# A two-layer hybrid block on one core: half-angle root in the recurrence, head 0 scored behind the last query slab, a semaphore for each half of a low part

## The chip, the cores and the metric

The kernel runs on one core of one Trainium2 chip. The metric is the device time of one execution in microseconds, lower is better; the time before is the median of 3 runs.

## The reference

Two layers over a sequence of 256 tokens and a context of 256 tokens, width 1024, all in fp32. Each layer modulates the RMS norm of its input, multiplies by one wide matrix, feeds four branches and merges them, then applies a SwiGLU feed-forward. The second layer carries only the 256 tokens through most of its work, since its context output is not needed.

```python
def _rglru_gates(u, wa, ba, wx, bx, lam):
    r = sigmoid(blockwise(u, wa) + ba);  i = sigmoid(blockwise(u, wx) + bx)
    log_a = -LRU_C * softplus(-lam) * r
    a = exp(log_a)
    b = sqrt(-expm1(2.0 * log_a)) * (i * u)
    return a, b                                   # then a linear scan h = a*h + b, both ways

def _window_attention(q, k, v, kc, vc, sink):     # 8 heads, 2 kv heads, blocks of 128, window 128
    p = softmax([local scores, context scores, sink])
    return p_local @ v + p_ctx @ vc
...
ys = (short_conv(...) @ w_a_out, attention(...) @ w_b_out,
      (gelu(r_g) * rec) @ w_c_out, conformer_conv(d_v, d_g) @ w_d_out)
out = (sum over n of sigmoid(gate_n) * ys_n) @ w_out
x = x + gt1 * out;  x = x + gt2 * swiglu(modulate(x))
```

## The kernel before

All matrices arrive as a stream of slabs of 1 MB: 128 partitions x (8 row tiles x 2 column tiles x 128). A layer has 104 slabs, in stages named c_in (8 slabs), kv (2), q (4), d_in (8), c_out, b_out, a_cu (8 each), a_b (4), a_out, d_out (8 each), w_out (4), then ff_in and ff_out in three parts. Slabs alternate between two slots `s`; `m` counts pairs.

Each fp32 product is made of three reduced-precision ones (fp32r). ScalarE copies the raw slab in two halves into a high part `WH` (`high`, semaphore `hi_done`), GpSimd (`low`, L416) or VectorE (`low`, `lows`) subtracts it from the raw slab into a low part `WL` (semaphore `lo_done`), and TensorE adds WH*HH, WH*HL and WL*HH (`products`, L441). A slab is 48 such matmuls, over 512 columns in the first layer, over 256 in most of the second. The slot of the raw slab is free for the next load when both halves of its low part are done. GpSimd makes both halves in every stage of the first layer and in the stages of `POOL_WHOLE`; elsewhere in the second layer GpSimd makes the first half and VectorE the second. In c_in VectorE makes both. `begin(m, s, halves)` is TensorE's wait before a slab: for one or both halves of the low part, and until the PSUM banks 2s and 2s+1 have been read (`slab_out`). With halves=1 the second half is waited for at k = 4 of the first tile. `in_order` allows halves=1 only where one engine makes both halves, since both raised one semaphore.

At the start, 8 slabs of modulation weights are loaded into buffers that are still free (S, S, RAW, TMP, G, G, CD, CD). TensorE turns each pair into modulation rows and columns and then runs two row tiles of slab 0.

In c_in, each slab gives a head of the recurrence (`front`: convolution and GELU). `gates(n)` multiplies by the gate matrices (8 plain fp32 matmuls). ScalarE then makes, over 512 columns, four Tanh for the gates, and `decays(n)`: Tanh, Exp and Exp again of multiples of the decay argument; VectorE forms (e+1)*tanh (`rests`), ScalarE its root (`roots`, which needs another activation table), VectorE two products, two scans (`scans`, L1415) and the output.

In kv and q, keys and queries are rotated: TensorE applies ROT to a copy (`rotate`, into banks 4 to 7), VectorE multiplies by cosine (`cosines`, which also frees the slab's banks) and sine (`turned`). The last head's scans (`scans(KC - 1)`) stand on VectorE ahead of the cosines of query slab 0.

In d_in, one head of attention runs beside each slab. TensorE's slab of 16 steps (3 matmuls each) is cut by a list: `("t0", 6)` puts the transposes of unit 0 after step 6, `o0` its product with V, `n0` the scores of unit 0 of the next head. Unit 0 and 1 are the two query blocks, unit 2 the context (first layer only). VectorE makes the maxima (`maxima`), sums and the scaling of the probabilities (L1180), ScalarE the exponentials (`probs`), the copies of the transposes, then at the slab's end the copy of the head's result, a Tanh and `high` of the slab after next. TensorE's `turn(n, 0)` (L681) waits for the scaling.

In a_out of the second layer, the layer norm of branch d runs between the pairs: mean and variance on TensorE, subtractions, scalings and gates on VectorE and ScalarE; its result is split into high and low parts (`z_low`) during the last pair.

Of the kernel before, what the change touches and what calls it, by code (L numbers as in the profile page):

```python
# [14 lines left out]
P = 128  # L15
# [55 lines left out]
POOL_WHOLE = ("c_in", "kv", "q", "d_in", "c_out", "b_out", "a_cu", "a_b", "a_out", "w_out")  # L71
# [34 lines left out]
ATTENTION = [[("t0", 6), ("t1", 9), ("o0", 9), ("t2", 13), ("o1", 13), ("n0", 14), ("o2", 16)],  # L106
# [16 lines left out]
def build(nc, stream, modw, lruw, xT, cT, prm, rope, consts, outT):  # L123
    with ExitStack() as ctx:
# [27 lines left out]
        LC = sb("LC", 3 * 16)  # L152
# [82 lines left out]
        lo_done = [sem(f"lo_done{s}") for s in range(2)]  # L235
# [13 lines left out]
        def stage_sems(l):  # L249
# [11 lines left out]
            st("lam_v", "pos den inv z z2 p6 p5 p4 p3 p2 p1 p0 log sp c0 c1 c2 hb")  # L261
# [7 lines left out]
            st("ci_a", "r0 r1 i0 i1 t0 t1 a0 a1 e0 e1")  # L269
# [78 lines left out]
        def _(sp):  # L348
# [22 lines left out]
            for l in range(DEPTH):  # L371
# [40 lines left out]
        def _(pool):  # L412
            def low(m, s, h):
# [3 lines left out]
                    .then_inc(lo_done[s], 1)  # L417
# [21 lines left out]
        def _(pe):  # L439
# [3 lines left out]
            def begin(m, s, halves=2):  # L443
                pe.wait_ge(lo_done[s], 2 * m + halves)
                pe.wait_ge(slab_out[s], m + 1)

            def second_half(m, s):
                pe.wait_ge(lo_done[s], 2 * m + 2)

            def in_order(l, name, first):  # L450

                i = [x for x, _ in STAGES].index(name)
                if first:
                    l, name = (l, STAGES[i - 1][0]) if i else (l - 1, STAGES[-1][0])
                return l <= 0 or name in POOL_WHOLE
# [41 lines left out]
            def stage(l, name, ops, nk=KC, before=None, pairs=None, ready=None):  # L497
# [5 lines left out]
                def pair(i, start):  # L503
                    for s in range(2):
                        slots = []
                        if start >= skip:
# [3 lines left out]
                             halves=1 if in_order(l, name, start == 0) else 2)  # L510
# [43 lines left out]
            def stage_and_sums(l, name, nk, before, after, nm, w, wo):  # L554

                b = pair_base(l, name)
                for n in range(4):
# [4 lines left out]
                         halves=1 if in_order(l, name, i == 0) else 2,  # L562
# [38 lines left out]
            for l in range(DEPTH):  # L601
# [26 lines left out]
                def rotate(st_a, st_p, n, s):  # L628
                    for t in range(2):
# [4 lines left out]
                        mm(bank(4 + 2 * s + t, NX), ROT, KR[t][:, 0:NX] if st_a is a["kv_a"] else QR[s][t], True, True).then_inc(st_p.sem, 1)  # L634
# [19 lines left out]
                b = pair_base(l, "q")  # L654
                slab(b, 0, [(H, W), (H, W)], halves=1)
                for n in range(1, 4):
# [1229 lines left out]
```

## Time and profile before

| | |
|---|---|
| median of 3 runs | 2160.63 us (2160.46 to 2161.41) |
| profiled execution | 2154.54 us, span 2152.7 us |
| TensorE matmul busy | 2072.0 us, 96% |
| TensorE weight load busy | 1720.3 us, 80% |
| VectorE, ScalarE, GpSimd busy | 1125.2, 907.0, 823.5 us |
| mean granted TensorE clock | 0.993 |
| HBM read | 275.80 MB |

The span is from the first to the last instruction; the execution's own time is 1.8 us longer. In a row of the timeline the first number is the start, the second the duration; the bracket at its end is the idle time of the engine ahead of it and what released it. Durations of a group of instructions overlap a little, so the start of the next row says more on pace than the sum. A granted clock of 1.00 is 2.4 GHz, of 0.50 1.2 GHz.

### The profile page before, as it was taken

How to read it: one execution, taken by the hardware profiler on the slowest of the kernel's cores; microseconds unless marked ns; L12 is line 12 of the kernel's file. 1: busy time of each engine (PE TensorE's matmuls, PEld its weight loads, DVE VectorE, ACT ScalarE, POOL GpSimd, SP SyncE). 2: the span in 40 equal slices, each digit the busy share in tenths (PEclk: the TensorE clock that was granted, in tenths of full speed). 3: DMA queues.
4: the chain of work that ended last, by engine and by line, in shares of the span. 5: the costliest groups of instructions: out<-in, count | busy, mean ns of one | idle time of the engine just before them, and what ended most of it. 6: DMA issues, size and time to landing. Idle time of an engine off the chain costs nothing.

```text
span 2152.7 us, 30915 instructions
## 1 busy us (share of the span) xinstructions
PE 2072.0 (96%) x11836; PEld 1720.3 (80%) x11836; DVE 1125.2 (52%) x2021; ACT 907.0 (42%) x1424; POOL 823.5 (38%) x348
## 2 busy tenths in 40 slices
PE   6999889999999999999999999999999999999997
PEld 4778677788877778776777778776889999899997
DVE  6894354577789532123111111489745886444555
ACT  4895333322222332233222212379755434544434
POOL 1003221344434334332333344400445887644443
PEclk9999999999999999999999999999999999999999
DMA  8212111222222222654534422421223555344443
GB/s 332 79 59 98 59 43 56 79 98 88 88 98 90 87 78 104 236 218 176 225 120 173 156 96 81 155 77 71 108 100 120 177 190 187 146 174 157 178 176 137
DMA packets 38699, 278.37 MB, mean 129 GB/s; under 512 B 4416, under 2 KB 4416, under 8 KB 5312
## 3 DMA queue, kind: packets, MB, share of 16 engines
q1 hardware_dynamic: 38592, 276.87, 35.1%
q8 instruction: 76, 1.25, 0.2%
q14 instruction: 31, 0.25, 0.0%
HBM read 275.80 MB, written 1.05 MB: 129 GB/s over the span
## 4 chain that ended last, share of the span: by engine, by line
PE 79%; DVE 9%; ACT 7%; issue 2%; DMA 2%; POOL 1%; SPq 0%; DVEq 0%; ACTq 0%; POOLq 0%
PE PS L441 76%; PE PS L524 2%; ACT WH L769 2%; DVE PS L1177 1%; ACT S L769 1%; DVE SM L1180 1%; ACT TMP L769 1%; ACT L769 1%; PE PS L681 1%; DVE WL L1174 1%; DVE ZL L1174 1%; ACT CD L769 1%; POOL WL L416 1%; DMA RAW<-in_stream 1%; DMA S<-in_modw 1%
## 5 line engine op out<-in xcount | busy, mean ns | idle before, releaser
L416 POOL TENSOR_TENSOR WL<-RAW,WH 128x1024 fp32r<-128x1024 f32 x344 | 823.3, 2413 | 1313.3 <-ACT WH L769 1313.3
L441 PE MATMUL PS<-HH,WH 128*128 128x512 f32 (+1 forms) x2272 | 807.7, 355 | 19.3 <-DVE HL L1177 7.3
L441 PE MATMUL PS<-HL,WH 128*128 128x512 f32 (+1 forms) x2272 | 780.2, 343 | 0.0
L441 PE MATMUL PS<-HH,WL 128*128 128x512 f32 (+1 forms) x2272 | 779.7, 343 | 0.0
L769 ACT ACTIVATE WH<-RAW 128x1024 fp32r<-128x1024 f32 x416 | 417.4, 1052 | 666.1 <-PE PS L441 626.4
L441 PEld LDWEIGHTS PS<-HH,WH 128*128 128x128 f32 x2272 | 430.2, 189 | 96.5 <-issue 30.0
L441 PEld LDWEIGHTS PS<-HL,WH 128*128 128x128 f32 x2272 | 430.5, 190 | 59.5 <-issue 7.9
L441 PEld LDWEIGHTS PS<-HH,WL 128*128 128x128 f32 x2272 | 429.7, 189 | 56.0
L441 PE MATMUL PS<-ZH,WH 128*128 128x512 f32 (+1 forms) x992 | 339.4, 342 | 10.7 <-DVE ZL L1174 7.1
L441 PE MATMUL PS<-ZL,WH 128*128 128x512 f32 (+1 forms) x992 | 336.1, 339 | 0.0
L441 PE MATMUL PS<-ZH,WL 128*128 128x512 f32 (+1 forms) x992 | 336.1, 339 | 0.0
L1177 DVE SCALAR_TENSOR_TENSOR PS<-G,PRM,PS 128x512 f32<-128x512 f32 (+1 forms) x464 | 254.5, 616 | 0.2
L441 PEld LDWEIGHTS PS<-ZH,WH 128*128 128x128 f32 x992 | 187.4, 189 | 39.1 <-DVE ZL L1174 9.0
L441 PEld LDWEIGHTS PS<-ZH,WL 128*128 128x128 f32 x992 | 187.3, 189 | 22.7
L441 PEld LDWEIGHTS PS<-ZL,WH 128*128 128x128 f32 x992 | 187.5, 189 | 22.0
L1174 DVE TENSOR_TENSOR TMP<-TMP,PS 128x512 f32<-128x512 f32 (+1 forms) x56 | 31.6, 564 | 291.4 <-ACT TMP L769 276.8
L769 ACT ACTIVATE TMP<-PS 128x256 f32<-128x256 f32 (+1 forms) x212 | 99.1, 468 | 198.3 <-PE PS L524 93.4
L1174 DVE TENSOR_TENSOR PS<-TMP,PS 128x256 f32<-128x256 f32 (+1 forms) x84 | 46.2, 550 | 198.1 <-ACT TMP L769 171.3
L1177 DVE SCALAR_TENSOR_TENSOR X<-PS,MOD,X 128x256 f32<-128x256 f32 (+1 forms) x96 | 41.6, 478 | 136.6 <-PE PS L441 136.5
L1174 DVE TENSOR_TENSOR WL<-RAW,WH 128x1024 fp32r<-128x1024 f32 x72 | 104.8, 1475 | 14.4 <-ACT WH L769 14.4
L441 PE MATMUL PS<-TMP,S 128*128 128x128 f32 (+2 forms) x288 | 64.4, 364 | 6.4 <-ACT S L769 3.6
L769 ACT ACT_TABLE_LOAD x49 | 62.9, 1283 | 1.6 <-PEq L1879 0.7
(157 smaller groups left out, 1572.1 us busy)
## 6 DMA issues: line engine op xcount, KB each, us to landing
RAW<-in_stream SPq DMA_DIRECT2D x208, 1024.0 KB, 4.8
CD<-in_modw SPq DMA_DIRECT2D x42, 1024.0 KB, 7.4
CD<-in_lruw SPq DMA_DIRECT2D x2, 2048.0 KB, 9.3
X<-in_xT SPq DMA_DIRECT2D x2, 1024.0 KB, 6.3
S<-in_modw SPq DMA_DIRECT2D x2, 1024.0 KB, 10.9
G<-in_modw SPq DMA_DIRECT2D x2, 1024.0 KB, 20.8
RAW<-in_modw SPq DMA_DIRECT2D x1, 1024.0 KB, 15.8
TMP<-in_modw SPq DMA_DIRECT2D x1, 1024.0 KB, 17.8
```

Source lines behind the costliest of these rows:

```text
L416: nc.gpsimd.tensor_tensor(WL[:, a:b], RAW[:, a:b], WH[:, a:b].bitcast(F32), ALU.subtract)\
L441: return nc.tensor.matmul(out, lhs, rhs, start=start, stop=stop)
L524: last = nc.tensor.matmul(PS[32 * g:32 * g + 32, 5 + slot, 0:2 * P], SILC[:, 32 * k:32 * k + 32], w[:, k * 2 * P:(k + 1) * 2 * P], start=k ...
L681: last = nc.tensor.transpose(bank(4 + u, P, q * P), PR[u % 2][:, q * P:(q + 1) * P], IDENT)
L769: return nc.scalar.activation(out, in_, f, **kw)
L1174: return V.tensor_tensor(out, x, y, op)
L1177: return V.scalar_tensor_tensor(out, x, sc, y, op0, op1)
L1180: return V.tensor_scalar(out, x, s1, s2, op0, op1) if op1 is not None else V.tensor_scalar(out, x, s1, None, op0)
```

## The change

1. *Half-angle root.* Before: tanh(x) from `lc(2)`, exp of twice the argument, (e+1)*tanh, root. After: t = tanh of half the argument, root of t straight away, and (a+1) times the weighted input (`sums` in place of `rests`); two Exp of 512 columns per head go. For the last head the product goes to PSUM (`driven`).
2. *Order of kv, q and head 0.* The last scans follow the cosines of query slab 0; rotations use halves of banks 6 and 7; head 0's copy and the Exp table are taken during query slab 3 (n == 2 on ScalarE), its units 0 and 1 are scored behind the last query slab, and their maxima and exponentials are made before the last rotations; the high part of d_in's slab 1 is taken behind them.
3. *Attention list of the first layer.* `n0` goes: all units of a head are scored ahead of its slab, and the other entries move back.
4. *Low parts.* `lo_done` has a semaphore for each half; all slabs begin with one half. `a_out` leaves `POOL_WHOLE`, so VectorE makes the second halves there in the second layer.
5. *a_out.* ScalarE takes a high part in the middle of the layer norm's gates, and gates slab 4 before the high part of the next slab.
6. *Start.* Constants, parameters, then X, then the first weight slab, then the modulation slabs; `decay(0)` and the first high part move ahead on ScalarE.

```diff
-POOL_WHOLE = ("c_in", "kv", "q", "d_in", "c_out", "b_out", "a_cu", "a_b", "a_out", "w_out")
+POOL_WHOLE = ("c_in", "kv", "q", "d_in", "c_out", "b_out", "a_cu", "a_b", "w_out")
-ATTENTION = [[("t0", 6), ("t1", 9), ("o0", 9), ("t2", 13), ("o1", 13), ("n0", 14), ("o2", 16)],
+ATTENTION = [[("t0", 8), ("t1", 10), ("o0", 11), ("t2", 13), ("o1", 14), ("o2", 16)],
              [("t0", 12), ("t1", 14), ("o0", 16), ("o1", 16)]]
...
-        lo_done = [sem(f"lo_done{s}") for s in range(2)]
+        lo_done = [[sem(f"lo_done{h}_{s}") for s in range(2)] for h in range(2)]
...
@@ SyncE
             sp.dma_start(CIN[:, :], cT).then_inc(in_loaded, 16)
+            sp.dma_start(CST[:, :], consts).then_inc(par_loaded, 16)
+            sp.dma_start(PRM[:, :], prm).then_inc(par_loaded, 16)
             for j in range(2):
...
-            sp.dma_start(CST[:, :], consts).then_inc(par_loaded, 16)
-            sp.dma_start(PRM[:, :], prm).then_inc(par_loaded, 16)
+            load(0, 0)
             for j, n in enumerate(MOD_ORDER):
                 sp.dma_start(MOD_HOMES[j], slab_of(modw, n)).then_inc(first_loaded[j // 2], 16)
-                if j == 1:
-                    load(0, 0)
...
-                                sp.wait_ge(lo_done[s], 2 * (i + 1))
+                                for h in range(2):
+                                    sp.wait_ge(lo_done[h][s], i + 1)
@@ TensorE
             def begin(m, s, halves=2):
-                pe.wait_ge(lo_done[s], 2 * m + halves)
+                for h in range(halves):
+                    pe.wait_ge(lo_done[h][s], m + 1)
                 pe.wait_ge(slab_out[s], m + 1)
...
-                             halves=1 if in_order(l, name, start == 0) else 2)
+                             halves=1)
...
-                        mm(bank(4 + 2 * s + t, NX), ROT, ...
+                        mm(bank(6 + s, NX, t * NX), ROT, ...
...
+                b = pair_base(l, "q")
+                slab(b, 0, [(H, W), (H, W)], halves=1)
+                for n in range(1, 4):
+                    slab(b + n // 2, n % 2, [(H, W), (H, W)], halves=1)
+                    if n == 1:
+                        pe.wait_ge(a["kv_v"].sem, a["kv_v"].at(0, "s1"))
+                    if n == 3:
+                        for u in range(2):
+                            scores(0, u, 0, 0)
+                        pe.wait_ge(a["q_v"].sem, a["q_v"].at(0, "s1"))
+                    rotate(a["q_a"], a["q_p"], n - 1, (n - 1) % 2)
+                pe.wait_ge(a["q_v"].sem, a["q_v"].at(1, "s1"))
+                rotate(a["q_a"], a["q_p"], 3, 1)
...
                     if n == 0:
-                        pe.wait_ge(a["q_v"].sem, a["q_v"].at(2, "s1"))
                         parts = [("s2", 4)] + parts if units == 3 else parts
-                    for u in range(units):
-                        if u == 1 or (n > 0 if u == 2 else n == 0 or not ahead):
+                    else:
+                        for u in range(units):
                             scores(n, u, kv, s)
@@ ScalarE
                 def roots(n):
                     for d in range(2):
-                        act.wait_ge(av.sem, av.at(n, f"w{d}"))
-                        fn(lru(n, 2 * d), lru(n, 2 * d), ACT.Sqrt).then_inc(a["ci_s"].sem, 1)
+                        act.wait_ge(aa.sem, aa.at(n, f"a{d}"))
+                        fn(lru(n, 2 * d), lru(n, 4 + d), ACT.Sqrt).then_inc(a["ci_s"].sem, 1)
...
-                    for d in range(2):
-                        act.wait_ge(aa.sem, aa.at(n, f"a{d}"))
-                        fn(lru(n, 2 * d), lru(n, 2 * d), ACT.Exp, scale=lc(1, n, d), bias=lc(1, n, d)).then_inc(aa.sem, 1)
...
                 for n in range(4):
                     tiles(b + n // 2, n % 2)
                     q_in(n, n % 2, b + n // 2)
-                    high(b + n // 2 + 1, n % 2)
+                    if n < 3:
+                        high(b + n // 2 + 1, n % 2)
                     if n == 0:
                         z_high(KC - 1)
-                table(ACT.Exp)
+                    if n == 2:
+                        act.wait_ge(a["q_v"].sem, a["q_v"].at(0, "s0"))
+                        stage_q(0, 0)
+                        table(ACT.Exp)
...
+                for u in range(2):
+                    probs(0, u)
+                high(b + 2, 1)
... layer norm of a_out
                 for k in range(KC):
                     act.wait_ge(lv.sem, max(lv.at(0, f"n{k}"), lv.at(0, f"s{k - 2}") if k > 1 else 0))
                     fn(bank(5 + k % 2, W), row(CD, k, W), ACT.Sigmoid, bias=par(l, "ln_b", k)).then_inc(la.sem, 1)
+                    if k == KC // 2:
+                        tiles(b, 0)
+                        high(b + 1, 0)
                 table(ACT.Sigmoid)
-                stage(l, "a_out", gate("ao"), some=(2, 3))
+                gate("ao")(4, 0, b)
+                tiles(b, 1)
+                high(b + 1, 1)
+                gate("ao")(5, 1, b)
@@ VectorE
-                def rests(n):
+                def sums(n):
                     for d in range(2):
-                        dve.wait_ge(aa.sem, aa.at(n, f"e{d}"))
-                        stt(lru(n, 2 * d), lru(n, 2 * d), 1.0, lru(n, 4 + d), ADD, MUL).then_inc(av.sem, 1)
+                        dve.wait_ge(aa.sem, aa.at(n, f"a{d}"))
+                        dve.wait_ge(av.sem, av.at(n, f"iu{d}"))
+                        x = lru(n, 2 * d + 1)
+                        stt(x, lru(n, 6 + d), 1.0, x, ADD, MUL).then_inc(av.sem, 1)
+                def driven(n, d):
+                    return bank(4 + d) if n == KC - 1 else lru(n, 2 * d + 1)
...
-                scans(KC - 1)
-                outputs(KC - 1)
-                for n in range(4):
...
+                for n in range(3):
+                    dve.wait_ge(tile_done[n % 2], 2 * (pair_base(l, "q") + n // 2) + 2)
+                    cosines(a["q_a"], a["q_v"], n, n % 2, lambda t: query(n, t))
                     if n == 0:
+                        scans(KC - 1)
+                        outputs(KC - 1)
                         z_out(KC - 1)
-                    turned(a["q_v"], a["q_p"], n, n % 2, lambda t: row(CD, 2 * n + t, NX))
+                    if n < 2:
+                        turned(a["q_v"], a["q_p"], n, n % 2, lambda t: query(n, t))
...
+                for u in range(2):
+                    maxima(0, u)
+                dve.wait_ge(tile_done[1], 2 * (pair_base(l, "q") + 1) + 2)
+                turned(a["q_v"], a["q_p"], 2, 0, lambda t: query(2, t))
+                cosines(a["q_a"], a["q_v"], 3, 1, lambda t: query(3, t))
+                turned(a["q_v"], a["q_p"], 3, 1, lambda t: query(3, t))
...
-                    if ahead and n + 1 < HEADS:
-                        maxima(n + 1, 0, par(l, "sink", n + 1))
... a_out, second layer (also behind gated(KC - 1, 1, b))
                 gated("ao")(KC - 2, 0, b)
+                if l == DEPTH - 1:
+                    low(b + 1, 0)
```

## Rows read from the trace of the kernel before

**Rows 1.** The page, part 1: busy time, share of the span, instructions.

```profile
PE 2072.0 (96%) x11836; PEld 1720.3 (80%) x11836; DVE 1125.2 (52%) x2021; ACT 907.0 (42%) x1424; POOL 823.5 (38%) x348
```

**Rows 2.** Timeline of TensorE at the start: start, duration, operation, count.

```profile
16.07 3.64 PE L524 MATMUL PS<-S,SILC 128*32 128x256 f32 x32 [0.76 <-DMA S<-in_modw]
...
23.45 1.08 PE L524 MATMUL PS<-RAW,SILC 128*32 128x256 f32 x8 [1.94 <-DMA TMP<-in_modw]
```

**Rows 3.** Waits of TensorE, 226 to 400 (total, times, longest); timeline at 230.

```profile
PE PS L681 <- DVE TMP L1180: 14.4, 8, 1.9
...
230.02 1.19 PE L441 MATMUL PS<-TMP,S 128*128 128x512 f32 x1 [3.59 <-ACT S L769]
```

**Rows 4.** Waits of TensorE, 1466 to 1572.

```profile
PE PS L441 <- DVE CD L1174: 6.8, 2, 4.0
PE PS L441 <- ACT TMP L769: 2.3, 2, 1.6
PE PS L441 <- ACT S L769: 1.6, 1, 1.6
PE PS L441 <- POOL WL L416: 1.3, 2, 0.7
```

**Rows 5.** Waits of TensorE, 1845 to 1873.

```profile
PE PS L441 <- DVE ZL L1174: 2.3, 2, 1.9
PE PS L441 <- POOL WL L416: 2.2, 3, 1.1
```

**Rows 6.** Waits of TensorE, 1990 to 2152.

```profile
PE PS L441 <- DVE WL L1174: 3.7, 7, 1.2
```

**Rows 7.** Windows: length, then busy PE, PEld, DVE, ACT, POOL, clock, DMA.

```profile
230.00:235.60 5.60, 5.58 (x9) 3.15 (x10) 2.96 (x10) 1.16 (x4) 1.64 (x1) 0.50 0.49 176
...
300.50:303.90 3.40, 3.40 (x11) 2.83 (x11) 1.35 (x6) 1.60 (x6) 0.00 (x0) 0.50 0.86 306
1549.80:1553.20 3.40, 3.40 (x17) 3.40 (x18) 2.25 (x7) 1.94 (x3) 2.32 (x1) 0.50 0.38 157
```

**Rows 8.** Timeline of TensorE in and behind head 2 of the first layer.

```profile
289.16 1.02 PE L441 MATMUL PS<-TMP,S 128*128 128x512 f32 x2
...
300.34 0.79 PE L681 MATMUL PS<-CST,TMP 128*128 128x128 f32 x3 [1.95 <-DVE TMP L1180]
```

**Rows 9.** Timeline of ScalarE and of GpSimd, same stretch.

```profile
292.50 0.60 ACT L769 ACTIVATE CD<-PS 128x512 f32<-128x512 f32 x1 [4.14 <-PE PS L441]
...
294.61 4.74 POOL L416 TENSOR_TENSOR WL<-RAW,WH 128x1024 fp32r<-128x1024 f32 x2 [15.21 <-ACT WH L769]
```

**Rows 10.** The chain that ended last, one slab of 48 matmuls.

```profile
620.73 11.52 PE PS L441 x48
```

**Rows 11.** Timeline of VectorE, same stretch, and its window over one unit's maxima.

```profile
297.07 2.30 DVE L1180 TENSOR_SCALAR SM<-SM 128x2 f32<-128x2 f32 x1
...
299.79 0.49 DVE L1180 TENSOR_SCALAR TMP<-TMP,SM 128x512 f32<-128x512 f32 x1
...
290.22:291.80 1.58, 1.48 (x5) 1.00 0.00 0
```

**Rows 12.** Second layer, c_in: two Exp on ScalarE, and one slab's window.

```profile
1448.77 1.52 ACT L769 ACTIVATE CD<-CD,LC 128x512 f32<-128x512 f32 x2
...
1464.90:1478.59 13.69, 12.95 (x61) 9.59 (x61) 12.87 (x20) 13.63 (x21) 0.00 (x0) 1.00 0.19 71
```

**Rows 13.** Second layer: scans of heads 6 and 7 on VectorE, GpSimd beside.

```profile
1526.82 2.33 DVE L1415 TENSOR_TENSOR_SCAN S<-S 128x512 f32<-128x512 f32 x2
...
1541.30 6.64 DVE L1415 TENSOR_TENSOR_SCAN TMP<-PADA,TMP 128x512 f32<-128x512 f32 x2
...
1541.00 5.85 POOL L416 TENSOR_TENSOR WL<-RAW,WH 128x1024 fp32r<-128x1024 f32 x2 [0.78 <-ACT WH L769]
```

**Rows 14.** Second halves of low parts on VectorE, without and with GpSimd beside.

```profile
1980.54 1.21 DVE L1174 TENSOR_TENSOR WL<-RAW,WH 128x1024 fp32r<-128x1024 f32 x1
...
1997.19 2.58 DVE L1174 TENSOR_TENSOR WL<-RAW,WH 128x1024 fp32r<-128x1024 f32 x1 [1.34 <-ACT WH L769]
```

More of the change, by code:

```diff
@@ L652, in _ @@
                 rotate(a["kv_a"], a["kv_p"], 0, 0)
-                b = pair_base(l, "q")
-                slab(b, 0, [(H, W), (H, W)], halves=1)
-                for n in range(1, 4):
-                    slab(b + n // 2, n % 2, [(H, W), (H, W)], halves=1)
-                    if n == 1:
-                        pe.wait_ge(a["kv_v"].sem, a["kv_v"].at(0, "s1"))
-                    rotate(a["q_a"], a["q_p"], n - 1, (n - 1) % 2)
-                pe.wait_ge(a["q_v"].sem, a["q_v"].at(1, "s1"))
-                rotate(a["q_a"], a["q_p"], 3, 1)
-                b = pair_base(l, "d_in")
                 units = 3 if l == 0 else 2
@@ new lines, in probs @@
+                def probs(n, u):
+                    sm = 14 * u
+                    act.wait_ge(dv.sem, dv.at(n, f"n{u}"))
+                    if u < 2:
+                        fn(PR[u], bank(4 + u), ACT.Exp, scale=SCALE, bias=SM[:, sm + 4:sm + 5],
+                           accum_out=SM[:, sm + 6:sm + 7]).then_inc(da.sem, 1)
+                    else:
+                        for q in range(2):
+                            fn(PR[0][:, q * NC:(q + 1) * NC], bank(6, NC, q * NC), ACT.Exp, scale=SCALE,
+                               bias=SM[:, sm + 4 + q:sm + 5 + q], accum_out=SM[:, sm + 6 + q:sm + 7 + q]).then_inc(da.sem, 1)
+                    act.wait_ge(dv.sem, dv.at(n, f"f{u}"))
+                    q = 2 if u == 2 else 1
+                    fn(SM[:, sm + 8:sm + 8 + q], SM[:, sm + 8:sm + 8 + q], ACT.Exp).then_inc(da.sem, 1)
@@ L1280, in _ @@
                 if l == 0:
+                    for s in range(2):
+                        dve.wait_ge(x_loaded[s], 16)
+                    sums, squared = a["n1_s"].sem, a["n1_a"].sem
+                    for k in range(1, KC):
+                        dve.wait_ge(squared, k + 1)
+                        if k > 1:
+                            dve.wait_ge(sums, k - 1)
+                        tt(tmp(1), tmp(1), SQUARES[k % 2], ADD).then_inc(sums, 1)
                     rows = G[:, :].rearrange("p (k n) -> p k n", n=GW)
@@ L1439, in _ @@
                     if n > 0:
-                        rests(n - 1)
+                        sums(n - 1)
                 z_out(KC - 3)
@@ L1444, in _ @@
                 weights(KC - 1)
-                rests(KC - 1)
+                sums(KC - 1)
                 z_out(KC - 2)
@@ L1526, in d_in_slab @@
-                    ahead = units == 3
+                    mx, mm_, nm, _, es, _, _ = scalars(u)
+                    dve.wait_ge(a["di_s"].sem, a["di_s"].at(n, f"s{u}"))
+                    if u < 2:
+                        far = bank(4 + u, P, (1 - u) * P)
+                        step(tt(far, far, TRI[u], ADD), f"k{u}")
+                        step(V.reduce_max(mx, bank(4 + u), AX.X), f"m{u}")
+                    else:
+                        step(V.reduce_max(mx, seqs(bank(6), 2), AX.X), "m2")
@@ L1527, in d_in_slab, with step @@
+                turned(a["q_v"], a["q_p"], 3, 1, lambda t: query(3, t))
+                def d_in_slab(n, s, m):
+                    def step(ins, name):
+                        ins.then_inc(dv.sem, 1)
+                        dve.wait_ge(dv.sem, dv.at(n, name))
                     for u in range(units):
-                        if u > 0 or not ahead or (isinstance(n, int) and n == 0):
-                            maxima(n, u, sink)
+                        if n > 0 or u == 2:
+                            maxima(n, u)
@@ L1547, in _ @@
                 b = pair_base(l, "d_in")
-                if units == 3:
-                    for n in range(KC):
-                        d_in_slab(n, n % 2, n // 2 + b)
-                else:
-                    with dve.Fori(0, KC // 2) as i:
-                        for s in range(2):
-                            d_in_slab(2 * i + s, s, i + b)
+                for n in range(KC):
+                    d_in_slab(n, n % 2, n // 2 + b)
                 def conv_d(taps):
@@ L1692, in _ @@
                 gated("ao")(KC - 1, 1, b)
+                if l == DEPTH - 1:
+                    low(b + 1, 1)
                 stage(l, "d_out", gated("do"), some=(0, 3))
```

138 lines of the change are left out of this document (50 added, 88 removed).

## The prediction

> **What bounds the kernel.** I read the page first: the matmul rows cover 2072.0 of the 2152.7 us span [rows 1]. The reader should see that nothing is gained by shortening another engine as such; what can be gained is the 80.7 us in which TensorE stands still, plus what it does at half clock. So I took the waits of TensorE stage by stage, then the timeline around the longest, then the windows for the clock.
>
> Five places matter to this change. (1) The start, to about 48 us: TensorE's first modulation matmuls begin at 16.07 when S has landed, and the next at 23.45 when TMP has landed [rows 2]. (2) The q and d_in stages of the first layer: 3.6 us until ScalarE has staged head 0, and 14.4 us in 8 waits for the scaled probabilities, together 18.0 us [rows 3]. (3) The second layer from the middle of c_in to head 0 of d_in: 6.8 + 2.3 + 1.6 + 1.3 = 12.0 us [rows 4]. (4) The end of a_out in the second layer: 2.3 + 2.2 = 4.5 us [rows 5]. (5) The rest of the second layer: 3.7 us for low parts made by VectorE [rows 6]. Besides, a stretch with the granted clock at 0.50 (1.2 GHz in place of 2.4) follows some waits: 5.6 us after the 3.6 us wait, 3.4 us in the attention loop at 300.5 and as much at 1549.8 [rows 7]. The record of the first layer's loop has a second such stretch near 362, and one stands at 1870.6, of 3.4 us each. Work at half clock takes twice its time, so I price a stretch at half its length: 2.8 and 1.7 us.
>
> **The change, part by part.**
>
> *Start.* X now follows two small loads and the first weight slab goes ahead of the first two modulation slabs. Between 16.07 and 23.45 three transfers of 1 MB land, 2.46 us each [rows 2]; so S lands 2.46 us later. Behind it stand the mod rows, the columns, VectorE's AMP, S and HH and the first slab, none with cover. X delayed by 0.8 MB (1.9 us) shifts the square sums and the reciprocal, which had some 2 us of room and now have 2.46 more. Taking the high part of slab 0 early is on no path. Cost 2.5 us; bounds 0 and 4.4 (both delays in full).
>
> *First layer, head 0.* ScalarE now stages head 0 and loads the Exp table while slab 3 of q runs, and TensorE scores units 0 and 1 right behind that slab. The 3.6 us wait goes, and the 2.8 us of half clock that followed. The new wait: slab 3 of q with its rotations ended at 230.02 - 3.59 = 226.4 [rows 3]. Two scores behind it (0.9 each), and the slab begins at 228.2; eight steps of 0.70 and the scores of unit 2 bring TensorE to t0 at 234.7. VectorE has the first scores at about 225.5: maxima of units 0 and 1 (1.58 each [rows 11]) to 228.6, then ten products of 0.4 for queries 2 and 3 to 232.5, then unit 2's reduction to 233.2. ScalarE has both exponentials by 229.3 and only then takes the high part of slab 1, so GpSimd works from 230.4 to 235.1, and VectorE's 128x2 instruction waits for it (below); the scaling ends 1.35 later, at 236.5. A wait of 1.9 us instead of 0.8.
>
> *First layer, heads 1 to 7.* Here is most of the sum. In head 3 TensorE arrived at t0 at 298.39 and stood until 300.34 [rows 8]. Counting from ScalarE's copy at 292.50 [rows 9], that is an arrival at 5.89. The change puts scores(n,0) in front of the slab instead of at step 14 (0.9 us from 289.16 to where the next step is regular [rows 8]) and moves t0 from step 6 to 8. Three matmuls of 0.24 us make a step [rows 10], say 0.70 as the starts near 289 show: arrival at 5.89 + 0.9 + 1.41 = 8.20. What did it wait for? VectorE's 128x2 TENSOR_SCALAR at 297.07 took 2.30 us, and ended as GpSimd's two WL instructions did (294.61 + 4.74 = 299.35); then came 0.9 us up to the end of the scaling that began at 299.79 [rows 9, 11]. In the new order VectorE makes the maxima of unit 0 (1.58 us [rows 11]) and unit 1 inside the head. From the gate product, which ends at 1.8, they end at 3.3 and 4.8, the reduction of unit 2 at 5.5; its first 128x2 instruction meets GpSimd and is let through at 6.85, when GpSimd ends. From there three small instructions instead of one go ahead: 1.35 us to the end of the scaling, at 8.20. Arrival and data meet; I take 0.07 us of wait a head. The look-ahead that is given up costs VectorE nothing, since it would have waited for GpSimd anyway. Later steps have room: t1 comes 1.8 us behind t0, its data 0.8 us behind. Idle 18.0 becomes 1.9 + 0.5 = 2.4, so 15.6 us; half clock 2.8 + 2 x 1.7 = 6.2 less 0.7 for what the new 1.9 us wait may bring: 5.5. Sum 21.1 us.
>
> So the trace shows VectorE held for the whole of a GpSimd instruction, 2.30 us. The Trainium skill (SBUF — State Buffer, "Who interferes with whom") says the same of an instruction in a two-port mode, and counts every `tensor_scalar` that meets the conditions among them; by it the scaling of 128x512 would be held too if GpSimd were still busy, which is rival (a).
>
> *Second layer, c_in.* ScalarE loses two Exp of 512 a head, 1.41 us (1.52 for the two, with 0.1 of overlap [rows 12]), and its roots no longer wait for VectorE. Its period was 13.69, nearly all busy (13.63); VectorE was busy 12.87 of it [rows 12], so VectorE becomes the slower at about 13.0, TensorE wants 11.9. The lag that made the waits grew by 1.8 us a slab and now grows by 1.1 from a later start, which leaves 1.3 us or more in front of each gate: the 3.9 us of waits go. VectorE's `sums` costs what `rests` did. In the first layer TensorE sets the pace there, and the change brings nothing.
>
> *Second layer, kv to head 0.* The lag gone, the V copy and the high part behind it come 5 us earlier: no wait for GpSimd (1.3). Cosines of query 0 now go ahead of the last scans, which frees its banks before the scans; that takes the 4.0 us wait, and scores behind slab 3 take 2.8. The last scans took 6.64 for two under GpSimd's work, against 2.33 for two without [rows 13]; their product now lies in PSUM. For a scan with one input in PSUM there is no row: between 1.17 and 3.32 us each. I take 1.17, since scalar_tensor_tensor with one PSUM input kept its time under GpSimd. At 3.32 each, slab 3 would wait 2.6 us. New wait: with the four waits gone, slab 3 of q ends near 1552.4 on the old clock; scores and two rotations of 0.9, slab from 1556.0, twelve steps at half the columns (0.36): TensorE reaches t0 at 1560.4. VectorE ends two maxima at 1556.3 and ten products at 1560.4; its scaling is due at 1560.8, but ScalarE's high part behind the exponentials has GpSimd busy from 1558.1, and its second half ends at 1562.8. The scaling ends at 1563.3: 2.9 us (bounds 0 and 4.7). Sum 12.0 - 2.9 = 9.1, and 1.7 of half clock at 1549.8, of which I count 1.0: 10.1 us.
>
> *a_out, second layer.* VectorE takes each second half from GpSimd. Such a half cost it 1.21 us alone and 2.58 beside GpSimd [rows 14]; 8 of them fit its idle time, but two lie on the chain of the layer norm, and ScalarE's high part in the middle of its gates adds up to 2 us, so the bank of slab 6 comes free about 1.0 us late, as before, and its second half 1.1 us late (before 0.7). GpSimd then has two halves instead of four beside the 8 z_lows, so these end 2.4 us earlier; the last 2.6 us of the 4.5 go. With a part of the stretch at 1870.6: 3.0 us; bounds -1 and 6.2.
>
> Each moved half therefore costs up to 2.58 us, and eight of them, overlapped and bare, 20.6 us; but VectorE stood idle over 4 us a slab there. The Trainium skill (SBUF — State Buffer, "Who interferes with whom") speaks against the edit: a VectorE instruction with two SBUF inputs contends with a GpSimd instruction that reads SBUF, and a low part is one.
>
> *halves=1 everywhere, own semaphores.* A slab starts when GpSimd's first half is ready. At the stage ends VectorE's half came 1.2 us behind GpSimd's, and is wanted 1.5 us into the slab. I take 2.7 of the 3.7 us [rows 6] (the last slab is held by its load); bounds 0 and 3.7.
>
> **Sum.** -2.5 + 21.1 + 10.1 + 3.0 + 2.7 = 34.4 us. The profiled execution took 2154.54 us (span 2152.7), 6.1 below the median of the runs, 2160.63. Its own time would become 2120.1; the median 2126.2.
>
> **Rivals.** (a) *A port wait remains in the loop.* If the scaling or a second 128x2 instruction is caught by one more GpSimd half (2.37 us) in each of 7 heads, 16.6 us and two half-clock stretches (3.4) come back: gain 14.4, 2146. Half of it: 2138. For it: arrival and data meet within 0.1 us, so any lateness shows; against: GpSimd ends at 6.85. (b) *The scan in PSUM is slowed.* 2.6 us and the half clock, 4.3 in all: 2130.5. (c) *Slower.* VectorE, with all maxima behind the head's start, loses the port to both GpSimd halves once more before the scaling: 4.74 us in 8 heads is 37.9, and 3.4 of half clock, against 34.4: 2167. It decides from 4.4 us of wait a head. Against it: GpSimd has only two halves a head, and they are over. (d) *Nothing arrives*: TensorE, early, meets the next late low part or load each time. Against it: before the loop of d_out slabs follow each other without waits. (e) *More*: z waits and other half-clock stretches vanish as well, 39 or more.
>
> **Numbers.** Forecast 0.62 (own range 2121 to 2132), (a) 0.15, (b) 0.08, (e) 0.08, (d) 0.04, (c) 0.03. The range 2118 to 2140 holds the first, (b), most of (e) and half of (a). 0.2%, 4.3 us, is about what the measurement can tell from no change: faster 0.93, within 0.03, slower 0.04.
>
> **What would show it.** The waits of TensorE between 226 and 400: one of about 1.9 us and seven under 0.3, heads every 18.1 us. S landing at 18.5. No wait for the gates in the second c_in. Two last scans at 2.3 us together. One wait of 3 us in the second layer's head 0. Wrong would be a t0 wait near 1 us or more in every head, or slabs of the second layer's a_out held by VectorE's halves.

## The result and the profile after

The changed kernel took 2108.89 us (median of 4 executions, 2108.26 to 2112.01), the kernel before 2160.61 beside it: a ratio of 0.9763, 95% interval 0.9746 to 0.978, or 51.7 us less. The forecast was 34.4 us less and a range down to 2118, so the direction was right and the size was not. Timed again in a later set the changed kernel took 2109.57 (2108.0 to 2111.2) against 2157.89, 48.3 us less. Over the 46 executions of the kernel before that the experiments brought, its median is 2157.9 (2154.0 to 2164.5); I use 2157.9 and, for the changed kernel, the median of its nine executions, 2109.0. The gain is then 48.9 us.

Part 1 of the page of the changed kernel answers to [rows 1]: the span is 45.5 us shorter, and of the 80.7 us in which TensorE stood still 49.1 are left.

```profile
span 2107.2 us, 30977 instructions
PE 2058.1 (98%) x11836; PEld 1716.8 (81%) x11836; DVE 1113.9 (53%) x2027; ACT 887.8 (42%) x1393; POOL 806.1 (38%) x340
```

TensorE's own busy time fell by 13.9 us too, although it does the same 11836 matmuls. Part of that is work at half clock, which counts as busy: by the mean granted clocks of the two profiles, 0.993 and 0.996, less half clock is worth some 7 us (an estimate). The modulation matmuls at the start took 2.2 us less between them. What the rest is no row here tells.

The waits of TensorE in the changed kernel (total, times, longest), for 226 to 400, which answers to [rows 3], and for the second layer from 1380 to 1560, to [rows 4]:

```profile
PE PS L665 <- DVE TMP L1185: 1.8, 1, 1.8
```

```profile
PE PS L441 <- DVE HL L1182: 3.4, 7, 2.1
PE PS L665 <- DVE TMP L1185: 3.1, 1, 3.1
PE PS L441 <- POOL WL L416: 0.3, 1, 0.3
```

The eight waits of the loop are one, the four kinds of wait of the second layer's c_in to head 0 are gone but for 0.3, and one new wait of 3.1 stands before the transposes. The row of 3.4 belongs to the start of that layer; it was 3.1 before.

One head of the first layer's loop, from the timelines of ScalarE, GpSimd, VectorE and TensorE, which answers to [rows 8, 9, 11]:

```profile
243.58 0.60 ACT L764 ACTIVATE CD<-PS 128x512 f32<-128x512 f32 x1 [3.27 <-PE PS L441]
```

```profile
245.69 4.76 POOL L416 TENSOR_TENSOR WL<-RAW,WH 128x1024 fp32r<-128x1024 f32 x2 [13.12 <-ACT WH L764]
```

```profile
249.08 1.40 DVE L1185 TENSOR_SCALAR SM<-SM,PRM 128x2 f32<-128x2 f32 x1
...
251.10 0.49 DVE L1185 TENSOR_SCALAR TMP<-TMP,SM 128x512 f32<-128x512 f32 x1
```

```profile
233.75 0.66 PE L665 MATMUL PS<-CST,TMP 128*128 128x128 f32 x4 [1.79 <-DVE TMP L1185]
...
251.65 0.66 PE L665 MATMUL PS<-CST,TMP 128*128 128x128 f32 x4
...
269.52 0.66 PE L665 MATMUL PS<-CST,TMP 128*128 128x128 f32 x4
```

The reader is to see three things. The 128x2 instruction is let through at 250.48, as GpSimd ends at 250.45. The scaling ends at 251.59, 8.0 us behind ScalarE's copy. TensorE comes at 251.65, so nothing is waited for, and the next head comes 17.87 us later; only head 0, at 233.75, waited.

### The profile page after: what moved, and what is told of

Its sections match the earlier page's. It is cut to its first block, busy times and chain, and to the rows that moved or that the text cites. A ratio compares the mean times of both kernels' runs of the same rounds, so it can differ in the third digit from the quotient of the medians.

```text
span 2107.2 us, 30977 instructions
## 1 busy us (share of the span) xinstructions
PE 2058.1 (98%) x11836; PEld 1716.8 (81%) x11836; DVE 1113.9 (53%) x2027; ACT 887.8 (42%) x1393; POOL 806.1 (38%) x340
## 4 chain that ended last, share of the span: by engine, by line
PE 89%; DVE 6%; ACT 2%; DMA 1%; issue 1%; POOL 0%; SPq 0%; DVEq 0%; ACTq 0%; POOLq 0%
PE PS L441 86%; PE PS L518 2%; DVE PS L1182 1%; ACT WH L764 1%; PE PS L665 1%; DVE ZL L1179 1%; DVE PS L1179 0%; DVE TMP L1185 0%; POOL WL L416 0%; DMA CD<-in_lruw 0%; DMA X<-in_xT 0%; DMA CD<-in_modw 0%; ACT TMP L764 0%; DVE HL L1182 0%; DVE PS L1275 0%
## 5 line engine op out<-in xcount | busy, mean ns | idle before, releaser
L416 POOL TENSOR_TENSOR WL<-RAW,WH 128x1024 fp32r<-128x1024 f32 x336 | 805.9, 2417 | 1286.3 <-ACT WH L764 1286.3
L1179 DVE TENSOR_TENSOR WL<-RAW,WH 128x1024 fp32r<-128x1024 f32 x80 | 117.4, 1484 | 15.4 <-ACT WH L764 15.2
L1182 DVE SCALAR_TENSOR_TENSOR G<-G,PS 128x512 f32<-128x512 f32 (+1 forms) x16 | 8.9, 556 | 103.2 <-ACT G L764 103.2
```

The costliest lines, as they stand in the source:

```text
L416: nc.gpsimd.tensor_tensor(WL[:, a:b], RAW[:, a:b], WH[:, a:b].bitcast(F32), ALU.subtract)\
L1179: return V.tensor_tensor(out, x, y, op)
L1182: return V.scalar_tensor_tensor(out, x, sc, y, op0, op1)
```

## The experiments

All times are medians of 5 executions or more; each set also timed the kernel before. Against 2109.0 for the changed kernel, a difference of under some 3 us is no more than the intervals can tell by itself, and I then look at the profile.

**The changed kernel again**, as the reference of its set, 2109.57.

> The changed kernel once more, on the chip that times the others of this set, as their reference. 2108.9 us if chips agree. Its executions so far spread over 3.8 us, those of the kernel before over 9.1 us (2155.1 to 2164.2); if the spread comes from stretches at half clock behind TensorE's waits, it stays narrow here, with a mean clock of 0.995 to 0.998 against 0.990 to 0.995 before.

The mean granted clock of its executions was 0.995 to 0.997, that of the kernel before 0.988 to 0.995 over all 46. The spread is narrower, as expected. That the clock makes the spread is not shown: over the 46 executions of the kernel before, time and clock hang together only weakly (correlation -0.34), over the nine of the changed kernel more closely (-0.84).

**The start.** Five kernels. The first two put it back in the changed kernel, without and with VectorE's order of waits (lines of the diff left out at the dots; `decay(0)` moves back too):

```diff
-            sp.dma_start(CST[:, :], consts).then_inc(par_loaded, 16)
-            sp.dma_start(PRM[:, :], prm).then_inc(par_loaded, 16)
             for j in range(2):
...
-            load(0, 0)
+            sp.dma_start(CST[:, :], consts).then_inc(par_loaded, 16)
+            sp.dma_start(PRM[:, :], prm).then_inc(par_loaded, 16)
             for j, n in enumerate(MOD_ORDER):
...
+                if j == 1:
+                    load(0, 0)
...
-            high(0, 0)
             norm_root(0, "n1", 2)
...
+                if p == 0:
+                    high(0, 0)
```

> The changed kernel with its start put back whole: X first, constants behind it, slab 0 behind two modulation slabs, its high part behind the first mod rows. By the prediction's step the start costs 2.5 us, so this should be 2.5 us faster than the changed kernel (2106.4), first slab of c_in done near 43. Theory that the new start gains (GpSimd's low part no longer beside VectorE's first AMP and S): 2.7 us slower (2111.6), the first wait behind slab 0 at 48.1 as before, AMP at 1.70 us for two and S at 3.66 for four.

> The changed kernel with every line of the start as before, VectorE's too: square sums do not wait for the parameters. In the earlier run of this set they did, which delayed the sums' matmul by 3.4 us and made TensorE wait 5.3 us, with a stretch at half clock. Prediction's step: 2.5 us faster than the changed kernel. Contention theory: the end of slab 0 at 48.1 as in the kernel before, against 45.5, so 2.7 us slower (2111.6).

The first took 2115.34, because of a fault of its own: VectorE waited for the parameters, which came last, and TensorE 5.3 us for mod rows. The second, the clean one, took 2110.89, 1.9 us more than the changed kernel. In its profile AMP and S take 1.70 and 3.65 us, as in the kernel before.

Only the high part moved back (the `high(0, 0)` lines of the diff above):

> The changed kernel, only the high part of slab 0 taken behind the first pair of mod rows again; loads in the new order. Contention theory: GpSimd's low part (4.7 us) lies beside AMP and S again, AMP 1.7 in place of 0.23 and S about 3.7 in place of 1.7, so 3 to 3.5 us slower than the changed kernel (2112). Theory that the order of the loads does it: no change (2109). The prediction's step put this edit at nothing.

It took 2114.58, 5.6 us more. Timelines of VectorE and GpSimd, first of this kernel, then of the changed kernel, where GpSimd is done when VectorE comes:

```profile
23.80 2.30 DVE L1183 SCALAR_TENSOR_TENSOR AMP<-MOD,PRM 128x2 f32<-128x2 f32 x2
26.13 3.64 DVE L1183 SCALAR_TENSOR_TENSOR S<-X,AMP,TMP 128x256 f32<-128x256 f32 x4
```

```profile
23.64 4.66 POOL L416 TENSOR_TENSOR WL<-RAW,WH 128x1024 fp32r<-128x1024 f32 x2 [23.19 <-ACT WH L764]
```

```profile
22.80 0.23 DVE L1182 SCALAR_TENSOR_TENSOR AMP<-MOD,PRM 128x2 f32<-128x2 f32 x2
23.07 1.67 DVE L1182 SCALAR_TENSOR_TENSOR S<-X,AMP,TMP 128x256 f32<-128x256 f32 x4
```

```profile
17.67 4.68 POOL L416 TENSOR_TENSOR WL<-RAW,WH 128x1024 fp32r<-128x1024 f32 x2 [17.22 <-ACT WH L764]
```

The same six instructions take 5.97 us from start to end when they begin beside GpSimd and 1.94 without it. TensorE then waited 5.45 us for them, and ran at half clock behind that wait:

```profile
30.70:36.40 5.70, 5.66 (x17) 4.85 (x18) 4.37 (x14) 1.86 (x5) 0.00 (x0) 0.50 0.83 339
```

(length, busy PE, PEld, DVE, ACT, POOL, granted clock, DMA). Only the load of slab 0 moved back:

> The changed kernel, only the load of slab 0 put back behind two modulation slabs (the high part keeps its new place on ScalarE, ahead of the root, so ScalarE now waits for that load there). Theory of the prediction: S lands 2.5 us earlier and the start gains up to 2.5. Contention theory: slab 0 lands about 2.5 us after S, ScalarE's root, mod rows and VectorE's AMP stand behind it, so no gain and up to 3 us of loss, GpSimd's low part ending after the first AMP again.

It took 2111.75, 2.7 us more; ScalarE's root stood behind the late slab, and TensorE waited 2.2 us for the mod rows. AMP took 0.23 us here: it came behind GpSimd's end.

Read together, these kernels separate the two halves of the new start. With the high part late, the new order of the loads took 2114.58 and the old one 2110.89, so the order by itself costs about 3.7 us (the two kernels differ in `decay(0)` and VectorE's order of waits too, and were timed in different sets). With the loads in the new order, the early high part gives back 5.6. With the old order it gives nothing (2111.75 against 2110.89), since ScalarE then waits for slab 0: the early high part needs the new order.

Last, the new start alone on the kernel before:

> The kernel before with the new start alone (order of the loads, decay and first high part early on ScalarE, VectorE's waits). Prediction's step: 2.5 us slower than the kernel before (2160.3). Contention theory: the end of slab 0 at 45.5 to 46.7 in place of 48.1 to 51.1, 1.3 to 3.3 us faster (2154.5 to 2156.5). An interval that holds both signs leaves it to the traces.

2154.52 against 2158.96, ratio 0.998, interval 0.9971 to 0.9989: 4.4 us faster (2.4 to 6.3). That the start as a whole is a cost is refuted. Its profile has AMP at 0.23 and S at 1.68, against 1.70 and 3.66 in the kernel before:

```profile
21.91 1.70 DVE L1177 SCALAR_TENSOR_TENSOR AMP<-MOD,PRM 128x2 f32<-128x2 f32 x2
23.64 3.66 DVE L1177 SCALAR_TENSOR_TENSOR S<-X,AMP,TMP 128x256 f32<-128x256 f32 x4
```

The profiles bear out only a part of the 4.4. TensorE's wait for CD behind slab 0 ends at 48.11 in the kernel before, at 46.67 with the new start alone, and at 45.45 and 46.74 in two executions of the changed kernel: 1.4 to 2.7 us earlier.

**The loop of the first layer alone**, on the kernel before (the last two lines in both engines, TensorE and VectorE).

```diff
-ATTENTION = [[("t0", 6), ("t1", 9), ("o0", 9), ("t2", 13), ("o1", 13), ("n0", 14), ("o2", 16)],
+ATTENTION = [[("t0", 8), ("t1", 10), ("o0", 11), ("t2", 13), ("o1", 14), ("o2", 16)],
-                ahead = units == 3
+                ahead = False
```

> The kernel before with the new attention list and all units of a head scored ahead of its slab in the first layer; nothing else. Prediction: the wait before the transposes of heads 1 to 7 falls from 1.95 to about 0.07, 13.2 us, and two stretches at half clock, 3.4 us; head 0 keeps its 3.6 us. Profile 16 us shorter, median 16 us shorter. Rival (a): waits near 1 us stay, gain under 10. If the kernel before loses more time to half clock in its other executions than in the profiled one, the gain between medians is 4 to 6 us larger than that between profiles.

2139.59 against 2157.89: 18.3 us faster (14.5 to 20.5). One wait is left between 226 and 400:

```profile
PE PS L441 <- ACT S L769: 3.6, 1, 3.6
```

**The transposes of unit 0 at step 6 again**, in the changed kernel: `("t0", 8)` becomes `("t0", 6)`.

> The changed kernel with the transposes of unit 0 after step 6 again in place of 8; nothing else. The scaling ends 8.0 us behind ScalarE's copy and TensorE would come at 6.8: seven waits of 1.3 us, 9 us of idle, and 1.3 more at head 0 (3.1). If idle is all that a wait costs, the median rises by 10.5 us, but two of the 8 steps it gives back come later without waits, so the head is 1.3 us longer: 2119.5 to 2120. If waits bring half clock in executions other than the profiled one, 2122 or more, and the mean clock of the executions falls from 0.996 to 0.993 or less.

2120.38, 11.4 us more, and 12.4 us of wait in place of 1.8:

```profile
PE PS L665 <- DVE TMP L1185: 12.4, 8, 3.2
```

Each of heads 1 to 7 waits 1.32 us. The cost is the idle time, 10.6 us, and no more than that can be read: the mean clock of the executions, 0.997, did not fall. So waits of this length did not bring more half clock on average. But the five executions lie 8.6 us apart, 2115.56 to 2124.15, and go with their clocks, 0.999 to 0.995 (correlation -0.95); whether such waits widen the spread stays open.

**The half-angle root alone**, on the kernel before (`rests` as `sums`, the second Exp out, `roots` from the tanh).

> The kernel before with the half-angle root alone (two Exp of 512 columns fewer a head, the root from the tanh, the product with (a+1)); no order changed. Prediction: the three waits of 3.9 us for the gates in the second layer's c_in go, and 1.3 us for GpSimd behind them, so about 5 us faster in the profile (2147.5 for the span); the waits of 4.0 and 2.8 us at query slab 0 and head 0 stay. Rival: the last scans under GpSimd give the time back, the 4.0 us wait grows by what was saved, and the gain is under 2 us.

2148.21 against 2157.64: 9.4 us faster (8.0 to 13.2). Waits of TensorE from 1410 to 1700:

```profile
PE PS L441 <- DVE CD L1171: 5.9, 2, 3.1
PE PS L441 <- DVE ZL L1171: 1.9, 1, 1.9
PE PS L441 <- DVE HL L1174: 0.5, 2, 0.2
```

Against [rows 4], the 3.9 us for the gates and the 1.3 for GpSimd are gone as forecast, and of the 6.8 us for VectorE's cosines 0.9 more. The rival that the scans take it back is out. In the profile the stretch from the layer's first wait to query slab 0 is 7.3 us shorter.

**Everything but the new order of kv, q and head 0**: start, root, list, semaphores and a_out put on the kernel before.

> All parts of the change but the new order of kv, q and head 0 (ScalarE's staging and table, scores behind slab 3 of q, cosines ahead of the last scans, rotations in banks 6 and 7, product in PSUM). Prediction: that order is worth 3.7 us in the first layer and 4.9 in the second, 8.6 in all, so 2118. If the parts add up as measured alone (1.3 + 18.3 + 9.4 + 3.2 + about 5), 2120 to 2121. If the waits before the gates and head 0 hang together, more than 12 us: above 2122. Waits of 3.6 us at head 0, about 3 and 2.8 at query slab 0 and head 0 of the second layer.

2118.18 us, 9.2 more than the changed kernel. It has 3.6 us of wait in the first layer's head 0, and 3.1 and 2.8 in the second layer:

```profile
PE PS L441 <- DVE CD L1171: 5.9, 2, 3.1
PE PS L441 <- DVE HL L1174: 3.5, 7, 2.1
```

**The last head's product in SBUF**, in the changed kernel: `driven` always returns `lru(n, 2 * d + 1)`.

> The changed kernel with the last head's product in SBUF, as in the other heads, so both inputs of its scans lie in SBUF. Prediction took 1.17 us for a scan with one input in PSUM beside GpSimd, 3.32 with both in SBUF. If so the two scans of the second layer take 5 to 6.6 us, VectorE's rotations and the banks of query slab 1 come 3 to 4 us later and TensorE waits 1 to 3 us: 1 to 4 us slower. If VectorE has that much room there, no change.

Last scans of the second layer, first of this kernel, then of the changed one; GpSimd runs beside them in both, here up to 1515.52, in the changed kernel up to 1514.16, when the scans end:

```profile
1513.20 4.51 DVE L1425 TENSOR_TENSOR_SCAN TMP<-PADA,TMP 128x512 f32<-128x512 f32 x2
```

```profile
1511.85 2.32 DVE L1425 TENSOR_TENSOR_SCAN TMP<-PADA,PS 128x512 f32<-128x512 f32 x2
```

2111.76, 2.8 us more, within what the intervals allow by chance; in the profile TensorE's waits for GpSimd there are 2.2 us in place of 0.3.

**a_out's low parts by GpSimd again**, in the changed kernel: `"a_out"` back in `POOL_WHOLE`, VectorE's two `low` calls out.

> The changed kernel with GpSimd making both halves of a_out's low parts in the second layer again; ScalarE's new order there stays. Prediction's step: 3.0 us of its gain lie in the whole a_out part, so up to 3 us slower (2112), waits for WL and for the z_lows back at the end of a_out, 2 to 4.5 us. If ScalarE's order does the work, no change. If the moved halves do it and more, 5 to 7 us slower (the part gained 6.65 between the profiles).

2112.8, 3.8 us more. From TensorE's wait at 1818.9 to the one at 1883.9 are 65.0 us; in the changed kernel the same two stand at 1816.8 and 1877.6, 60.7 us apart: 1.9 us wait for the low parts of the layer norm, and a stretch at half clock behind them.

```profile
1837.27 0.39 PE L441 MATMUL PS<-ZH,WH 128*128 128x256 f32 x1 [1.88 <-DVE ZL L1179]
```

**Both halves awaited**, in the changed kernel: `halves=2` again for slabs outside `POOL_WHOLE` in the second layer.

> The changed kernel, but a slab of the second layer's other stages waits for both halves of its low part before it starts, as before. Prediction's step: 2.7 us slower (bounds 0 and 3.7). If the semaphores for each half are worth what this part gained in the profile (4.6 us from 1904 on) plus the new VectorE halves in a_out, 5 us or more slower, with waits for WL by VectorE of 0.4 to 1.2 us each.

2114.43, 5.4 us more. Waits from 1940 to the end (the profile puts them down to issue):

```profile
PE PS L441 <- issue: 3.7, 5, 1.2
PE PS L441 <- DVE ZL L1186: 0.6, 1, 0.6
```

In the changed kernel the waits of the same stretch are 1.0, 0.7 and 0.2. Between 1560 and 1904, where a_out and d_out lie, the waits of the two kernels are the same: 3.6, 0.7 and 0.2 us.

**A better version**: the changed kernel with the high part of d_in's slab 1 ahead of head 0's exponentials.

```diff
-                    if n < 3:
-                        high(b + n // 2 + 1, n % 2)
+                    high(b + n // 2 + 1, n % 2)
...
                 for u in range(2):
                     probs(0, u)
-                high(b + 2, 1)
```

> A variant of the changed kernel: the high part of d_in's slab 1 is taken in the loop over q, ahead of head 0's exponentials, in place of behind them; nothing else. GpSimd is then done before VectorE's 128x2 instruction of unit 2. If GpSimd's two halves (4.76 us) hold that instruction, the wait of 1.79 us before the transposes of head 0 falls under 0.5, the one of 3.15 in the second layer to about 1, and the stretch at half clock behind it may go: 3 to 6 us faster (2104). If head 0 is late because of VectorE's own queue (maxima and ten products), the waits stay within 0.5 us: 2109 or above.

2104.12 (2101.68 to 2105.0), 4.9 us faster than the changed kernel and the fastest here. In the second layer the wait of 3.1 us is 1.0, since the scaling of the probabilities is no longer caught. VectorE and GpSimd there, first in the changed kernel, then in this one:

```profile
1534.89 2.33 DVE L1185 TENSOR_SCALAR TMP<-TMP,SM 128x512 f32<-128x512 f32 x1
```

```profile
1532.25 4.69 POOL L416 TENSOR_TENSOR WL<-RAW,WH 128x1024 fp32r<-128x1024 f32 x2 [5.67 <-ACT WH L764]
```

```profile
1533.20 0.49 DVE L1183 TENSOR_SCALAR TMP<-TMP,SM 128x512 f32<-128x512 f32 x1
```

```profile
1526.79 4.75 POOL L416 TENSOR_TENSOR WL<-RAW,WH 128x1024 fp32r<-128x1024 f32 x2 [1.61 <-ACT WH L764]
```

In the first layer unit 2's 128x2 instruction takes 0.23 us where it took 2.08, and the wait at head 0 is gone. The stretch of 6.8 us at half clock behind the second layer's wait went with it; in the second profiled execution of the changed kernel that stretch was 3.4 us.

## Why the prediction was right in direction and wrong in size

The parts, in us of gain between medians; a part that was taken out of the changed kernel counts with what that cost. The forecast's terms are sorted by these parts, and none is changed:

| part | forecast | measured |
|---|---|---|
| start | -2.5 | 4.4 alone, 1.9 when taken out |
| loop of the first layer, heads 1 to 7 and head 0's small wait | 17.4 (13.2 + 0.8 + 3.4) | 18.3 |
| half-angle root | 5.2 (3.9 + 1.3) | 9.4 |
| order of kv, q, head 0 | 8.6 | 9.2 |
| a_out's low parts by VectorE | 3.0 with ScalarE's order | 3.8 |
| one half at a slab's start | 2.7 | 5.4 |

The measured parts add up to 48.0 to 50.5, against 48.9 for the whole: so the parts are nearly independent, as far as intervals of some 3 us each can tell. ScalarE's new order in a_out was not timed by itself. The forecasts add up to 34.4.

**The failed step is the start.** The prediction said: "Taking the high part of slab 0 early is on no path. Cost 2.5 us". It put the early high part at nothing, so nothing stood against the 2.5 us for the late first pair; that was wrong, and with it the sign; this is the largest error, 4.4 to 6.9 us. The high part was on the path through the low part that it lets loose. In the kernel before GpSimd ran from 21.18 to 25.84, beside AMP and S, and made them 3.4 us longer; taken early, its low part is over before they start, which is worth 5.6 us in the changed kernel. I had the price of two SBUF inputs beside GpSimd in the text, for a_out, and did not look for it where a GpSimd instruction would be moved away. The experiment with the high part alone shows the mechanism, 5.97 us against 1.94; the start alone shows the sign.

The other half of the step, the cost of the new order, was about right. TensorE's own wait took up the delay: in [rows 2] it waited 1.94 us for the fifth transfer of 1 MB, slab 0 is among the first five in either order, and in the changed kernel the wait was 0.52. But VectorE's AMP follows the first pair and began at 23.80 with the high part late, against 21.77 with the old order; the medians put the order at 3.7 us, for 2.5 with bounds 0 and 4.4. How much of the profiles' gain is clock is not separated: the 16 matmuls from RAW took 1.93 us in the kernel before, 1.07 in the changed kernel, and 1.93 in the changed kernel's second profiled execution.

**Mis-sized: the root.** The forecast took 3.9 and 1.3 us and the profile confirms both. It left out that the earlier end of c_in takes 0.9 us from the wait for the cosines, and another 1.2 us went that no listed wait accounts for. That makes 7.3 in the profile, which lies below the interval of the medians (8.0 to 13.2); where the last 2 us, to the median of 9.4, come from is not settled.

**Mis-sized: one half at a slab's start.** Forecast 2.7 of the 3.7 us in [rows 6]; measured 5.4 in the median, 4.4 of them in the profile behind 1904. I took off 1.0 us for a half that is wanted 1.5 us into the slab, and that deduction was wrong. The listed waits differ by 2.6 us; what makes the other 1.8 of the 4.4 is open. It is not a_out or d_out, where the waits are the same.

**Right: the loop.** Arrival 8.20 us behind ScalarE's copy was forecast for both TensorE and the scaling; it was 8.07 and 8.01. Seven waits of 1.95 became none. The head came every 17.9 us, not 18.1. Rival (a), a port wait that remains, is out: GpSimd ended before anything but the 128x2 instruction met it, as the count of its two halves said. Head 0's wait was 1.79 for 1.9, and its cause the one named, as the better version shows.

**Right: kv to head 0 in the second layer.** The two scans took 2.32 us, for 2.3 forecast, and 4.51 with both inputs in SBUF, so rival (b) is out and the bound of 3.32 each was too high for this place. The wait at head 0 was 3.15 for 2.9. But I counted 1.0 us of gain at half clock, and in the changed kernel's profile a stretch of 6.8 us followed that wait where 3.4 had been (3.4 again in its second execution): this part gave 8.7 us between the profiles, not 10.1. Rival (c) never came near: no head but head 0 waits.

**a_out** gave 6.65 us between the profiles for 3.0 forecast: all of the 4.5 us in [rows 5] went, not 2.6, and the stretch at half clock near 1870 as well. VectorE's eight halves cost TensorE nothing; one wait of 0.7 us is left. The median says 3.8 for the halves alone.

**Two slips of the sums.** Half of rival (a) is 10.0 us less gain, which gives 2136 and not 2138, and head 0's wait, from 234.7 to 236.5, is 1.8 us and not 1.9. Neither moves the forecast by more than 0.1 us.

**The base.** I carried the 6.1 us between the profiled execution and the median over unchanged. Only three of the 46 later executions of the kernel before are faster than its profiled one, 2154.54, and their median is 3.4 us above it; that of the changed kernel, 2109.01, is at its median. So 2.7 us of the 51.7 is luck of the first executions, and about 3 us is a real difference that the two profiles do not show. The granted clock points the same way (mean 0.991 in the kernel before, 0.993 in its profile, 0.996 after), and 0.002 of the span would be some 4 us, an estimate, so it fits in size. At a correlation of -0.34 it does not settle it, and the experiment with waits of 1.3 us, whose mean clock did not fall, speaks against idle time as its cause. What lengthens the other executions of the kernel before stays open.

## What to carry to other kernels

Look at what a moved instruction sets off on a third engine: a high part on ScalarE is cheap, but its low part on GpSimd about tripled the time of six VectorE instructions on the path. When a transfer is put ahead of others, follow what each delayed one lets loose: here TensorE's own wait took up the delay, and VectorE's chain behind the first pair did not. Counting the arrival of data and of the engine from one common event, here ScalarE's copy, was right within 0.2 us.

## What the runs showed of the hardware

A VectorE instruction with two SBUF inputs was slowed by GpSimd's low part even where it touches two columns: two AMP instructions 0.23 us without it, 1.70 to 2.44 beside it. A scan of 512 columns took 1.16 us with one input in PSUM beside GpSimd and 2.25 with both in SBUF (the mean of two, the first 2.32 us of 4.51 beside GpSimd). The scaling of 128x512, with one SBUF tensor, took 0.49 us, but 2.33 when GpSimd's instruction was already running; it ended at 1537.22, GpSimd's at 1536.94. The Trainium skill (SBUF — State Buffer, "Who interferes with whom") has all three as rules: one SBUF input outside the two-port modes does not contend, two do with a GpSimd instruction that reads SBUF, and `tensor_scalar` in such a mode is held for the whole instruction. These traces agree; whether the scaling ran in such a mode they do not show.

Before the scaling, `TENSOR_SCALAR` of one column beside GpSimd kept 0.15 to 0.22 us, and the one of two columns, which came next, took 1.40.

The granted clock does not show every stretch at half pace. In the profile of the start put back whole, with VectorE's waits, the matmuls of 512 columns of slab 0 come 0.42 us apart from 29.8 to 34.9, for 0.23 in the kernel before, while the granted clock of these windows reads 1.00:

```profile
30.39 0.63 PE L442 MATMUL PS<-HL,WH 128*128 128x512 f32 x1
30.81 0.63 PE L442 MATMUL PS<-HH,WL 128*128 128x512 f32 x1
```

```profile
29.47 0.40 PE L441 MATMUL PS<-HL,WH 128*128 128x512 f32 x1
29.70 0.40 PE L441 MATMUL PS<-HH,WL 128*128 128x512 f32 x1
```

I had not expected how far a kernel of one core spreads: 10.5 us over 46 executions of the kernel before (9.1 and 7.2 over two sets of nine), against 4.0 us over nine of the changed one.
